# A hybrid 4-layer model on one core: Hyena's inverses, the keys' normalization, the last branch and the address of the transposed x are moved

## What is computed

```python
# first stack, each of 2 layers
x = x + 0.5 * swiglu(rmsnorm(x))
q, k, v, z, beta, alpha, hy_in = split(rmsnorm(x) @ w_in)
q, k, v = split(silu(dwconv(concat(q, k, v))))      # 5 taps
q, k = l2norm(q) * 128 ** -0.5, l2norm(k)           # 4 heads of 128
o_dn = rmsnorm(delta_rule(q, k, v) + flip(delta_rule(flipped))) * silu(z)
v, x1, x2 = split(dwconv(hy_in) + bias)             # 3 taps, 512 channels each
zz = v
for gate, h in ((x1, h1), (x2, h2)):
    zz = gate * (irfft(rfft(zz) * rfft(h)) + skip * zz)
x = x + concat(o_dn, rmsnorm(zz)) @ w_out
x = x + 0.5 * swiglu(rmsnorm(x))
# second stack, each of 2 layers
y = gates[0] * (o_da @ w_da) + gates[1] * (o_ret @ w_ret) + gates[2] * (o_sc @ w_sc)
x = x + y @ w_out
x = x + ffn(rmsnorm(x))
```

## Time and profile before

| | |
|---|---|
| median of 3 runs | 2048.61 us (2048.6 to 2050.78) |
| the profiled execution | 2050.59 us, its span 2048.8 us |
| granted clock of PE, mean | 0.997 |
| PE busy | 2005.7 us (98%) |
| POOL busy | 1490.3 us (73%) |
| ACT busy | 1039.1 us (51%) |
| DVE busy | 951.1 us (46%) |
| DMA, mean | 161 GB/s |

### The profile page before, as it was taken

One profiled execution on the slowest core, in us unless ns is written; L12 is line 12 of the kernel. 1 busy time (PEld: TensorE's weight loads), 2 busy tenths in 40 slices (PEclk: granted clock), 3 DMA queues, 4 the chain that ended last, 5 costly groups with the idle time before them and its releaser, 6 DMA issues.

```text
span 2048.8 us, 37047 instructions
## 1 busy us (share of the span) xinstructions
PE 2005.7 (98%) x15795; PEld 1847.8 (90%) x15795; DVE 951.1 (46%) x1587; ACT 1039.1 (51%) x1549; POOL 1490.3 (73%) x652
## 2 busy tenths in 40 slices
PE   7999999999999999999999999999999999999998
PEld 7998778989989998878899989999999899999997
DVE  3560766435204550766344204745476028345760
ACT  5443446564446444446464537456644374556442
POOL 6789445458887789445368887768788977687886
PEclk9999999999999999999999999999999999999999
DMA  6756233035555656233135565545455645455553
GB/s 220 237 181 210 94 108 116 27 124 185 186 193 178 220 176 208 91 103 103 44 124 186 186 224 165 164 146 185 163 175 181 206 156 161 143 187 172 181 184 134
DMA packets 250965, 329.10 MB, mean 161 GB/s; under 512 B 9008, under 2 KB 225586, under 8 KB 250418
## 3 DMA queue, kind: packets, MB, share of 16 engines
q1 hardware_dynamic: 250802, 326.73, 48.9%
HBM read 325.66 MB, written 1.05 MB: 159 GB/s over the span
## 4 chain that ended last, share of the span: by engine, by line
PE 60%; DVE 2%; issue 1%; ACT 1%; POOL 0%; DVEq 0%; ACTq 0%
PE psA L409 12%; PE psA L410 12%; PE psA L411 12%; PE psB L409 5%; PE psB L411 5%; PE psB L410 5%; PE psB L1934 1%; PE psA L1776 1%; PE psA L1777 0%; PE psA L2104 0%; PE psA L1782 0%; PE psA L2106 0%; DVE small L1518 0%; PE psB L2094 0%; PE psA L1888 0%
## 5 line engine op out<-in xcount | busy, mean ns | idle before, releaser
L1020 POOL TENSOR_TENSOR w_lo<-raw,w_hi 128x1024 fp32r<-128x1024 f32 x600 | 1457.6, 2448 | 525.6 <-ACT w_hi L596 524.0
L409 PE MATMUL psA<-xT_hi,w_lo 128*128 128x256 f32 x3168 | 909.2, 287 | 3.5 <-POOL w_lo L1020 1.5
L410 PE MATMUL psA<-xT_lo,w_hi 128*128 128x256 f32 x3168 | 896.2, 283 | 0.0
L411 PE MATMUL psA<-xT_hi,w_hi 128*128 128x256 f32 x3168 | 896.2, 283 | 0.0
L596 ACT ACTIVATE w_hi<-raw 128x1024 fp32r<-128x1024 f32 x600 | 629.9, 1051 | 371.2 <-PE psB L411 240.8
L409 PEld LDWEIGHTS psA<-xT_hi,w_lo 128*128 128x128 f32 x3168 | 607.5, 192 | 14.7 <-issue 9.6
L410 PEld LDWEIGHTS psA<-xT_lo,w_hi 128*128 128x128 f32 x3168 | 607.7, 192 | 3.4 <-issue 3.3
L411 PEld LDWEIGHTS psA<-xT_hi,w_hi 128*128 128x128 f32 x3168 | 607.5, 192 | 0.0
L1166 DVE TENSOR_TENSOR hT_lo<-hfull,hT_hi 128x256 fp32r<-128x256 f32 x132 | 245.3, 1893 | 1.2 <-ACT hT_hi L729 0.6
L409 PE MATMUL psB<-w_hi,hT_lo 128*128 128x512 f32 x528 | 205.6, 389 | 0.4 <-issue 0.4
L410 PE MATMUL psB<-w_lo,hT_hi 128*128 128x512 f32 x528 | 205.4, 389 | 0.0
(11 more groups left out here) (440 smaller groups left out, 2288.2 us busy)
## 6 DMA issues: line engine op xcount, KB each, us to landing
raw<-in_w_in SPq DMA_DIRECT2D x78, 1024.0 KB, 5.1
raw<-in_ffn_w_gate SPq DMA_DIRECT2D x44, 1024.0 KB, 5.1
raw<-in_ffn_w_up SPq DMA_DIRECT2D x44, 1024.0 KB, 5.1
raw<-in_ffn_w_down SPq DMA_DIRECT2D x44, 1024.0 KB, 4.9
raw<-in_w_ffn_in SPq DMA_DIRECT2D x44, 1024.0 KB, 4.9
raw<-in_w_ffn_out SPq DMA_DIRECT2D x22, 1024.0 KB, 4.8
raw<-in_w_out SPq DMA_DIRECT2D x16, 1024.0 KB, 4.8
raw<-in_w_branch_da SPq DMA_DIRECT2D x4, 1024.0 KB, 4.8
```

Source lines behind the costliest of these rows:

```text
L409: nc.tensor.matmul(o, a_lo, b_hi, start=start, stop=False, skip_group_check=skip)
L410: nc.tensor.matmul(o, a_hi, b_lo, start=False, stop=False, skip_group_check=skip)
L411: return nc.tensor.matmul(o, a_hi, b_hi, start=False, stop=stop, skip_group_check=skip)
L1020: nc.gpsimd.tensor_tensor(split_half(w_lo, n, kind), raw_half(n, kind), split_half(w_hi, n, kind).bitcast(F32), ALU.subtract)\
```

## The change

1. `xT_hi` and `xT_lo` move behind the arena, with a new tensor `line` of 16 elements (64 bytes) between. The arena moves down by 16 KB, the tables behind it up by 64 bytes.
2. On PE the first `hyena_inverse` follows projection 15 instead of 14, the second spectrum projection 16 instead of 15, the second inverse projection 20 instead of 19. DVE's spectral products and gates follow, as do ACT's squares of zz, logarithms, exponentials and the scaling of zz.
3. The exponential of the roots and the normalization become two instructions each, keys (`4:8`) first, and `key_products` waits for the keys alone ahead of its first two banks and for the queries ahead of the other two.
4. The two memsets of `U` move from the start of `deltanet` to behind the second gate.
5. The third branch goes bank by bank (`last_branch`): both halves for a bank, then the next bank. DVE subtracts a bank's rounded part between the gating and the addition of the next, and ACT's rounding of weights is spread over the banks.

```diff
-        xT_hi = sb("xT_hi", [P, KC, L], F32R)
-        xT_lo = sb("xT_lo", [P, KC, L], F32R)
         ARENA = 107 * KB
         slab = sb("slab", [P, ARENA // 4])
         at0 = nc.sbuf_base - ARENA
+        sb("line", [P, 16])
+        xT_hi = sb("xT_hi", [P, KC, L], F32R)
+        xT_lo = sb("xT_lo", [P, KC, L], F32R)
...
-                    if i == 20:
+                    if i == 21:
                         for rb in range(RB):
...
-                    if i == 21:
                         A(stat[:, 46:47], eps, ACT.Ln, bias=eps)
+                    if i == 22:
...
-                    if i == 22:
+                    if i == 23:
                         act.wait_ge(ch.sem, ch.step(l))
-                        A(rr[:, :, :], rr[:, :, :], ACT.Exp, scale=-0.5).then_inc(s1["qk_root"].sem, 1)
+                        for v in (slice(4, 8), slice(0, 4)):
+                            A(rr[:, v, :], rr[:, v, :], ACT.Exp, scale=-0.5).then_inc(s1["qk_root"].sem, 1)
...
-                    if i == 23:
+                    if i == 24:
...
-                for k in range(8):
+                for k in range(7):
                     round_half(1, l, 50 + k + AHEAD)
...
-                    if b in (0, 2):
-                        round_half(1, l, 58 + b // 2 + AHEAD)
+                    if b < 3:
+                        round_half(1, l, 57 + b + AHEAD)
...
-                    if i in (11, 12, 15, 16):
-                        spectral_product(l, i // 15, (i + 1) % 2)
-                    if i in (14, 19):
-                        hyena_gate(l, i // 19, 0)
-                        hyena_gate(l, i // 19, 1)
+                    if i in (11, 12, 16, 17):
+                        spectral_product(l, i // 16, (i + i // 16 + 1) % 2)
+                    if i in (15, 20):
+                        hyena_gate(l, i // 20, 0)
+                        hyena_gate(l, i // 20, 1)
+                    if i == 20:
+                        for d in range(DIRS):
+                            V.memset(U[BL * (1 - d):BL * (2 - d), 2 * d:2 * d + 2, :, BL * d:BL * d + BL], 0.0)
...
-                dve.wait_ge(s1["qk_root"].sem, s1["qk_root"].due(l, 1))
-                V.tensor_tensor(qkvT[:, 0:8, :], qkvT[:, 0:8, :], rr[:, :, :], ALU.mult).then_inc(s1["qk_norm"].sem, 1)
+                for n, v in enumerate((slice(4, 8), slice(0, 4))):
+                    dve.wait_ge(s1["qk_root"].sem, s1["qk_root"].due(l, n + 1))
+                    V.tensor_tensor(qkvT[:, v, :], qkvT[:, v, :], rr[:, v, :], ALU.mult).then_inc(s1["qk_norm"].sem, 1)
...
-                        dve.wait_ge(ch.sem, ch.step(l))
+                        gated = ch.step(l)
+                        if r == 2 and b:
+                            split_y(l, b - 1)
+                        dve.wait_ge(ch.sem, gated)
...
-                            if b:
-                                split_y(l, b - 1)
                 split_y(l, 3)
...
                     if i == 14:
                         turn_hyena(l, 4)
-                        hyena_inverse(l, 0)
                     if i == 15:
                         turn_hyena(l, 5)
+                        hyena_inverse(l, 0)
+                    if i == 16:
                         hyena_spectrum(l, 1)
-                    if i == 19:
+                    if i == 20:
                         hyena_inverse(l, 1)
...
+            def last_branch(l, k):
+
+                for i in range(2):
+                    pe.wait_ge(lo_done[1].sem, lo_done[1].due(l, 50 + k + i + 1))
+                for m, b in enumerate(bank_order[2]):
+                    pe.wait_ge(s2["br"].sem, s2["br"].due(l, bank_order[0].index(b) + 1))
+                    for i in range(2):
+                        hi, lo = split_half(w_hi, 50 + k + i, "B"), split_half(w_lo, 50 + k + i, "B")
+                        for c in (2 * b, 2 * b + 1):
+                            v = slice(c * P, (c + 1) * P)
+                            ins_ = product(psA[:, b, (c % 2) * L:(c % 2 + 1) * L], hi[:, v], lo[:, v], xT_hi[:, k + i, :],
+                                           xT_lo[:, k + i, :], i == 0 and c % 2 == 0, i == 1, skip=True)
+                        if m == 3:
+                            ins_.then_inc(half_used[1].sem, 1)
+                    if m < 3:
+                        ins_.then_inc(s2["br_mm"].sem, 1)
```

More of the change, by code:

```diff
@@ L375, in emit @@
             z_mm=8, y_spec=4, inv_mm=4, zz=4, hy_ss=2, hy_zn=1, hy_back=2, y_hi=8, y_lo=4,
-            qk_sq=1, qk_mm=1, qk_root=1, qk_norm=1, kv_turned=4, kv_nat=4,
+            qk_sq=1, qk_mm=1, qk_root=2, qk_norm=2, kv_turned=4, kv_nat=4,
             g_arg=1, g_exp=1, g_sum=1, g_ln=1, g_ready=1, g_cum=1, g_col=1, g_decays=1,
@@ L1393, in deltanet @@
                 g = lambda a, b: small[:, a:b]
-                for d in range(DIRS):
-                    V.memset(U[BL * (1 - d):BL * (2 - d), 2 * d:2 * d + 2, :, BL * d:BL * d + BL], 0.0)
-                dve.wait_ge(s1["qk_root"].sem, s1["qk_root"].due(l, 1))
-                V.tensor_tensor(qkvT[:, 0:8, :], qkvT[:, 0:8, :], rr[:, :, :], ALU.mult).then_inc(s1["qk_norm"].sem, 1)
+                for n, v in enumerate((slice(4, 8), slice(0, 4))):
+                    dve.wait_ge(s1["qk_root"].sem, s1["qk_root"].due(l, n + 1))
+                    V.tensor_tensor(qkvT[:, v, :], qkvT[:, v, :], rr[:, v, :], ALU.mult).then_inc(s1["qk_norm"].sem, 1)
                 four = lambda ps: ps.rearrange("p (h n) -> p h n", h=4)
@@ L2043, in key_products @@
             def key_products(l):
-                pe.wait_ge(s1["qk_norm"].sem, s1["qk_norm"].due(l, 1))
                 for n in range(4):
@@ L2048, in key_products @@
                     t = slice(c * P, (c + 1) * P)
+                    if c == 0:
+                        pe.wait_ge(s1["qk_norm"].sem, s1["qk_norm"].due(l, n // 2 + 1))
                     if n == 3:
@@ L2291, in stack2_mixer @@
                     x_hi, x_lo = (daT_hi, daT_lo) if r == 0 else (xT_hi, xT_lo)
+                    if r == 2:
+                        last_branch(l, k)
+                        continue
                     for i in range(n):
@@ L2297, in stack2_mixer @@
                                 pe.wait_ge(s2["ev_dve"].sem, s2["ev_dve"].due(l, 41))
-                            if i == 0 and r == 2:
-                                pe.wait_ge(s2["br"].sem, s2["br"].due(l, bank_order[0].index(b) + 1))
                             for c in (2 * b, 2 * b + 1):
-                                o = (psA, psB, psA)[r][:, b, (c % 2) * L:(c % 2 + 1) * L]
+                                o = (psA, psB)[r][:, b, (c % 2) * L:(c % 2 + 1) * L]
                                 v = slice(c * P, (c + 1) * P)
```

## The result

The changed kernel takes 2014.8 us (median of 4 runs, 2014.21 to 2016.84), the kernel before on the same chip 2049.7 (median of 4). The ratio is 0.9826, with a 95% interval of 0.9813 to 0.9838: 34.9 us less, where I had forecast 15.3 less. The time lies in the range of 2010 to 2045, but more than half of the gain was not in the sum. The profiled execution took 2016.84 us, with a span of 2014.9.

What follows compares the result with a forecast made beforehand. PE, busy for 98% of the span, was taken as the bound, so only its waits or own work could shrink. Savings of 5.4 + 2.9 + 5.1 + 1.9 = 15.3 us took 2048.6 to 2033.3 us; range 2010 to 2045.

Steps and rivals of the forecast that it cites:

- The inverse: Hyena's inverse one projection later: PE's 2.72 us wait for DVE's spectral product goes to zero in both layers, 5.4 us.
- Keys first: Ahead of the key products: the 2.96 us normalization wait shrinks to 1.5 us, for ACT's zz scaling; 2.9 us saved.
- both of my ends: DVE's keys' half of the normalization: 1.8 us if it scales with elements, 3.5 us at worst.
- The lowered clock: Behind waits at the inverse and key products: three clock falls go, 1.7 us each, 5.1 us saved.
- The branch: Last branch bank by bank: PE's 1.45 us wait for y's low part shrinks by 0.9 us per layer, 1.9 us.
- The address: Transposed x's new place: the large products' step stays 0.12 us, worth zero, with ends of -64 and +64 us.
- My rival: Transposed x's new place shortens the large products: about 1970 us at 113 ns, 2012 at a third of that; 20%.
- The case where it hurts: Even chunks of transposed x cross a 2 KB boundary, stopping reads for 13 ns: 63 us slower, about 2096; 6%.

Runs made afterwards that it cites:

- the first experiment: The kernel before with only the transposed x moved behind the arena and 64 bytes, work order unchanged: 2033.93 us, ratio 0.9916.
- the order alone: The changed kernel with the transposed x back at its old place ahead of the arena: 2035.55 us, ratio 0.9925.
- the 448-byte kernel: The changed kernel with a line of 448 instead of 64 bytes ahead of the transposed x: 2006.16 us (median of 4), ratio 0.9779.
- the 1088-byte kernel: The changed kernel with a line of 1088 instead of 64 bytes ahead of the transposed x: 2015.36 us, ratio 0.9826.
- the 192-byte kernel: The changed kernel with a line of 192 instead of 64 bytes ahead of the transposed x: 2009.2 us.

## Why the prediction was right, and where it was wrong

**The inverse** (5.4 us): right. The wait is gone, nothing is late in its place, and the memsets of `U` cost nothing where they stand now.

**Keys first** (2.9 us, a new wait of 1.5 us): right, and the mechanism is the one worked out. ACT and PE in the changed kernel, against the earlier trace rows:

```profile
932.82 2.01 ACT L825 ACTIVATE rr<-rr 128x1024 f32<-128x1024 f32 x2
...
936.04 1.32 ACT L830 ACTIVATE zz<-zz,small 128x512 f32<-128x512 f32 x2
```

```profile
937.41 0.66 PE L2045 MATMUL psA<-mats,zz 128*128 128x128 f32 x4 [1.44 <-ACT zz L830]
937.91 0.60 PE L2045 MATMUL psB<-mats,zz 128*128 128x128 f32 x4
938.34 3.74 PE L2059 MATMUL psB<-qkvT 128*128 128x128 f32 x32
```

PE waits 1.44 us for zz, and the key products follow the transposes without a wait. The normalization did better than both of my ends (1.8 and 3.5 us for a half). Against the earlier trace rows:

```profile
933.92 2.36 DVE L1402 TENSOR_TENSOR qkvT<-qkvT,rr 128x1024 f32<-128x1024 f32 x2 [0.34 <-ACT rr L825]
```

The two halves together take 2.36 us where the whole took 3.51. POOL in the kernel before and in the changed one shows what was different around them:

```profile
950.30 11.60 POOL L1020 TENSOR_TENSOR w_lo<-raw,w_hi 128x1024 fp32r<-128x1024 f32 x4 [2.23 <-ACT w_hi L596]
```

```profile
935.95 4.87 POOL L1022 TENSOR_TENSOR w_lo<-raw,w_hi 128x1024 fp32r<-128x1024 f32 x2 [2.31 <-ACT w_hi L597]
```

The whole ran beside a POOL without a pause; the halves ran from 933.92 to 936.28, and POOL stood idle from 933.64 to 935.95. So the better time may come from POOL's pause and not from the split. By the rule of the Trainium skill (SBUF — State Buffer, Who interferes with whom) on the shared port pair each half could wait behind a POOL instruction; this place does not test it.

**The lowered clock** (5.1 us): right. The changed kernel has no fall before its last microsecond. With the long waits put back and the new address kept (the first experiment), all four were followed by one. The length of a wait alone does not decide it: before, the inverse's wait was 2.55 us with a fall in one layer and 2.56 us without one in the other, and the first experiment has a wait of 2.58 us with none behind it:

```profile
101.52 0.36 PE L410 MATMUL psA<-xT_hi,w_lo 128*128 128x256 f32 x1 [2.58 <-POOL w_lo L1021]
```

Falls aren't bound to these places: the kernel with the order alone has one behind a wait of 2.07 us in the delta rule at 987 us, and the 448-byte kernel one behind a wait of 1.93 us at 100 us:

```profile
100.37 0.36 PE L410 MATMUL psA<-xT_hi,w_lo 128*128 128x256 f32 x1 [1.93 <-POOL w_lo L1022]
```

```profile
101.69:105.10 3.41, 3.41 (x18) 3.41 (x17) 1.74 (x2) 0.18 (x1) 3.41 (x2) 0.50 0.30 63
```

So waits of about 2 us can be followed by a fall, too; I had counted them only behind the long ones. Of the 14 waits of 1.82 to 2.10 us in the traces of all runs, past the first 20 us, eight were followed by one and six were not, among these one of 1.98 us in the kernel before.

**The branch** (1.9 us): nearly right. Against the earlier trace rows, the wait has gone from 1.45 to 0.71 us, which makes 1.5 us for two layers. DVE subtracts at 1401.09 with the addition of the next bank behind it:

```profile
1401.09 0.69 DVE L1548 TENSOR_TENSOR yT_lo<-psA,yT_hi 128x512 fp32r<-128x512 f32 x1 [0.20 <-ACT yT_hi L968]
1401.69 0.69 DVE L1681 TENSOR_TENSOR psA<-yacc,psA 128x512 f32<-128x512 f32 x1
```

```profile
1401.92 0.47 PE L410 MATMUL psB<-w_hi,yT_lo 128*128 128x512 f32 x1 [0.71 <-DVE yT_lo L1548]
```

The four terms by these rows are 5.4 + 3.0 + 5.1 + 1.5 = 15.0 us, and the order alone measured 15.6.

**The address** (0 us): wrong. This is the step that failed: the term that I put at nothing measured 20.2 us with the new order in place and 17.3 us alone. I argued from the earlier trace rows, where weights of 16 columns at eight distances all give 113 ns, that the excess over the columns follows the width of the weights and not their distance to x. The row was right and the conclusion did not follow from it. Its eight distances are multiples of 64 bytes, and at such distances narrow weights have 113.3 to 113.5 ns in every kernel here but one (114.5 with 192 bytes), while wide ones go from 119.9 down to 116.0; so narrow weights cannot show how the excess of wide ones depends on the distance. At other distances even they depend on it: 115.5 to 115.7 ns with lines of 160, 208 and 480 bytes and 117.5 with 32. The 128-column weights, which are the ones that count, stood at only one distance in the trace of before. There the trace was silent, not in favour of zero. My rival had the right sign and, with "a third of 64 us" and 2012, nearly the right time; its chance of 20% was too low for a case on which no row bore. That the time lies in my range at all is owed to this rival, for which the range went down to 2010, and not to the sum. The case where it hurts was refuted with its mechanism: even chunks, which cross a 2 KB boundary, have the step of odd ones.

**What the faster products cost in turn.** I had not asked what comes next when a step of PE takes 2.4 ns less. In the feed-forward parts PE now stands ahead of POOL's low weights for 4.1 us in all, where the earlier trace rows have 1.5 and the order alone has 1.2. The list names POOL, but the longest of these waits leads on, here PE, POOL, ACT and DVE of the changed kernel:

```profile
100.97 0.36 PE L410 MATMUL psA<-xT_hi,w_lo 128*128 128x256 f32 x1 [1.78 <-POOL w_lo L1022]
```

```profile
98.45 7.46 POOL L1022 TENSOR_TENSOR w_lo<-raw,w_hi 128x1024 fp32r<-128x1024 f32 x3 [3.95 <-ACT w_hi L597]
```

```profile
97.01 0.42 ACT L721 ACTIVATE sg<-gs 128x256 f32<-128x256 f32 x1 [8.09 <-DVE gs L1144]
97.33 1.04 ACT L597 ACTIVATE w_hi<-raw 128x1024 fp32r<-128x1024 f32 x1
```

```profile
87.43 4.80 DVE L1168 TENSOR_TENSOR hT_lo<-hfull,hT_hi 128x256 fp32r<-128x256 f32 x2
92.16 0.53 DVE L1201 TENSOR_SCALAR farg<-psB,cols 64x256 f32<-64x256 f32 x1
...
96.36 0.28 DVE L1212 TENSOR_SCALAR farg<-farg 64x256 f32<-64x256 f32 x1
96.57 0.74 DVE L1144 TENSOR_TENSOR gs<-psA,root_row 128x256 f32<-128x256 f32 x2
```

DVE is without a pause from 87.43 on: two low parts of h, then the arguments (`farg`) of the Hyena filter's sine, and only then the scaled gate `gs`. ACT's rounding of the next weights stands behind its use of `gs`, POOL's subtraction behind the rounding, PE behind the subtraction. DVE's work did not get shorter, so a PE that arrives earlier waits for it. Here it even got longer. The same two low parts before:

```profile
88.12 3.39 DVE L1166 TENSOR_TENSOR hT_lo<-hfull,hT_hi 128x256 fp32r<-128x256 f32 x2
```

PE waited 0.20 us at this place before and started at 100.29. Of the 1.58 us more, 0.9 are PE's earlier arrival and 0.7 the later data. The second of the long waits for POOL, 1.36 us at 697, has the same idle 3.95 us of POOL ahead of it.

**The books of the address.** The changed kernel against the order alone: 9504 x 2.43 = 23.1 us for the large products; 288 products of 256 columns that have the transposed x as weights (their columns come in two parts) by 4.2 ns, 1.2 us; less 192 x 5.8 ns = 1.1 us for those with x as weights; less 2.9 us for these waits. Together 20.3, and measured are 2035.55 - 2015.36 = 20.2 us on one chip. There the 1088-byte kernel stands for the changed one; with its own waits for POOL, 3.0 us, the sum would be 21.4. Nothing of the size of the difference is left over.

## What to carry to other kernels

Where the step of back-to-back matmuls is longer than their columns, try the distance between the streaming operand and the weights: a few bytes of padding ahead of one of them, at several lengths and on both sides, since neither the sign nor the size can be read off. Measure by the step in the trace, by role, since the same padding helps one shape and hurts another. And when a price is taken from the nearest row, ask whether that row could have shown the effect at all; if it could not, the row is no evidence for zero.

## What the runs showed of the hardware

- **float32r products of 128 x 128 weights by 256 columns:** 119.9 ns a step with both operands on one 256-byte grid, 116.9 at +32, 117.5 at +64, 118.9 at 128, 118.2 to 118.3 at -96, -48 and -32, and 116.0 at -64 bytes (address of the streaming operand less that of the weights, modulo 256), the last a mixture of 113.3 and 117.8 ns. All 110 changes between these two in the two executions of one kernel came at a break in the stream. At 2.4 GHz 256 columns are 106.7 ns, so 13.2 ns over become as few as 6.6.
- **The same with 512 columns** go the other way: 226.8 to 227.7 ns on the grid, 229 to 230 with the streaming operand 64 bytes past the weights, 232.6 to 233.3 at other distances. With 192 such products against 9504 that hardly counts here; for the 1584 of the temporary tensors it comes to 3.5 to 5.7 us, and to 8.2 us (232.0 ns) with the low weights alone moved.
- **The clock:** all falls to 1.2 GHz but one (6.83 us, with a wait of 4.21 us in the 192-byte kernel) and those at the very end last 3.41 us, which costs 1.7 us. They came behind all four waits of 2.7 to 3.0 us in one kernel, behind three of four of 2.6 to 2.8 in another, and behind eight of 14 waits of 1.82 to 2.10 us; waits of 2.58 us in one kernel and of 2.32 in another had none behind them.
- **Open:** why the distance acts, why -64 allows the short step of 113.3 ns in some stretches and what starts it. If all products of this kernel went at it, another 9504 x (116.0 - 113.3) ns = 26 us would be gained on paper, less what DVE and ACT then hold up.
